# Two norms and the memory values of a decoder layer, reordered around one ring of weight slots

## The chip, the cores and the metric

The kernel runs on one core of a Trainium2 chip. A core has a matrix engine (PE; its weight loads, PEld, overlap its matmuls), a vector engine (DVE), an activation engine (ACT), a general engine (POOL, which here only issues transfers and clears buffers), and a queue (SP) that issues transfers. The engines run apart and wait for each other on semaphores. The metric is the device time of one execution in microseconds (us), median of several runs.

## The reference, cut to what matters

One decoder layer for 256 prompt tokens and 8 sample tokens (T = 264 columns), width 2048. Three sub-layers, each `x <- x + RMSNorm_post(f(RMSNorm_pre(x)))`:

```python
def rmsnorm(x, g):
    x32 = x.astype(F32)
    y = x32 * lax.rsqrt(jnp.mean(x32 * x32, axis=-1, keepdims=True) + EPS) * g.astype(F32)

def memory_kv(mem, g, w_xkv):
    kv = jnp.einsum('bmd,dn->bmn', rmsnorm(mem, g), w_xkv)
    return kv.reshape(B_, M, 2, X_HEADS, X_HEAD_DIM)

def cross_attn(h, mem_kv, w_xq, w_xo):
    q = jnp.einsum('btd,dn->btn', h, w_xq).reshape(B_, T, X_HEADS, X_HEAD_DIM)
    ...
x = x + rmsnorm(y, n_mix_post)
x = x + rmsnorm(cross_attn(rmsnorm(x, n_x_pre), mem_kv, w_xq, w_xo), n_x_post)
y, new_conv = conv_ffn(rmsnorm(x, n_ffn_pre), w_up, conv_w, conv_b, w_down, conv_hist)
```

The divisor of a norm (one number per token) can be applied before a projection or, since the projection is linear, to its result.

## The kernel before

All projections use fp32 numbers split into a high and a low part (fp32r): a product is three matmuls, high by high, high by low, low by high (lines 572 to 574 of `product`). The 2048 features lie on 128 partitions in 16 tiles (KB = 16), tokens in columns. Weights pass through a ring of three buffers (RING = 3), one *slot* of 1 MB (16 blocks of 128 x 128) each, some 400 slots in a fixed order. For each slot SP loads the raw numbers, ACT makes the high part in two halves (`split_hi`, line 537), DVE the low part in two halves (`split_lo`, line 545), and PE runs its 48 matmuls. The splits for slot s + 3 are issued once slot s has been projected, at a place in the ACT and DVE programs that is written by hand. Every engine's program is in order, so an instruction that waits holds back all behind it.

Three stretches matter here.

*The first norm* (after `mix_out`, before cross attention). PE sums the squares of the mixer's output over partitions with a matrix of ones (`norm`, line 1907), then runs three slots of memory keys (PH_KA). DVE takes the divisor (`rstd`), makes the new residual in groups of four tiles, ACT squares each tile into a ring of three buffers, and PE adds up each square with one full-width fp32 matmul (`norm_sum`, line 1911) between the blocks of the second key slot. Only after that second divisor does DVE multiply the residual by it (line 2638) and ACT and DVE split it into `h_hi` and `h_lo`. The first query slot (PH_XQ 0) waits tile by tile for `h_lo`.

*Cross attention*. A list (X_WORK) puts the pieces of the attention behind the slots u = 0 to 22: 8 query slots, 13 slots of keys and values (PH_KB). Each key or value tile comes out as features by tokens and is turned by PE (`kv_turn`, one tile behind its slot) and copied by DVE (line 2656) into `kvtok2`, token rows that the output needs and that the product with the probabilities reads (pieces "oo").

*The second norm* (before the MLP) already works on the undivided residual: DVE and ACT make `x`, `h_hi`, `h_lo` two tiles at a time, PE runs slots 0 and 1 of the up-projection side by side, tile after tile, with a square's sum (`square_sum`, line 2072, 32 output partitions at 32 * (t % 4)) after each tile from the sixth, and from the eleventh on the third slot ten tiles behind (LAG = 10). The divisor multiplies the results (line 2798). Squares lie in a ring of nine. Ahead of this norm's first sum stand 16 transposes of the convolution's history and their four DVE copies (line 2755).

## Time and profile before

| | |
|---|---|
| median of 3 runs | 2647.24 us (2646.9 to 2647.4) |
| the profiled execution's own time | 2646.98 us, its span 2645.3 us |
| PE busy | 2572.2 us, 97% of the span |
| PEld, DVE, ACT busy | 2483.0, 1601.2, 1254.8 us |
| mean granted PE clock | 0.991 of full |

The span runs from the first to the last instruction; the 1.7 us between it and the execution's time lie around it. A matmul's shown length (0.28 us) is longer than the distance between the starts of two (0.12 us), since they are pipelined: rates are read from starts. A row of a stretch gives its bounds and length, then the busy time (and instructions) of PE, PEld, DVE, ACT and POOL, the granted PE clock as a share of full, the busy share of the transfer engines and GB/s.

### The profile page before, as it was taken

The page shows a single profiled execution, that of the slowest core. Times are in us where ns is not written, and L with a number is a line of the kernel's source. Part 1 is how long each engine was busy: PE and PEld are TensorE (multiplying, and loading weights), DVE is VectorE, ACT ScalarE, POOL GpSimd, SP SyncE. Part 2 cuts the span into 40 slices and gives each one's busy share as a digit, 9 for nine tenths or more (in the row PEclk, how much of TensorE's full clock was granted, in tenths as well). Part 3 has the DMA queues.
Part 4 walks back from the last instruction along what each step waited for, and adds up shares of the span by engine and source line. Part 5 has one row for each costly group of instructions (what it writes and reads, how often), then busy time and mean ns, then how long its engine had stood idle before and what let it go on. Part 6 is the DMA issues. An engine that isn't in the chain of part 4 may idle for free. (4 is left out here: it accounts for less than half of the span.)

```text
span 2645.3 us, 53817 instructions
## 1 busy us (share of the span) xinstructions
PE 2572.2 (97%) x20841; PEld 2483.0 (94%) x20841; DVE 1601.2 (61%) x2439; ACT 1254.8 (47%) x1948; POOL 196.3 (7%) x307
## 2 busy tenths in 40 slices
PE   7999999999999999999999999998999999999997
PEld 5988998999999999999999998987999999999997
DVE  4556565544565555555654657546777765777766
ACT  5465555433444444443443644435545555545553
POOL 1112111000111111100000001410000000000000
PEclk9999999999999999999999999999999999999999
DMA  6789789666888888866666656954566577666563
GB/s 201 217 256 282 235 259 294 173 179 191 238 233 233 234 232 230 222 186 184 175 177 206 189 147 190 306 190 128 144 182 183 151 192 198 175 184 180 157 187 108
DMA packets 855053, 530.96 MB, mean 201 GB/s; under 512 B 13961, under 2 KB 832065, under 8 KB 854135
## 3 DMA queue, kind: packets, MB, share of 16 engines
q1 hardware_dynamic: 822583, 440.07, 60.6%
q0 software_dynamic: 27312, 86.50, 9.4%
q10 hardware_dynamic: 5032, 2.62, 0.4%
q8 instruction: 91, 1.49, 0.2%
q14 instruction: 35, 0.29, 0.0%
HBM read 499.79 MB, written 33.29 MB: 202 GB/s over the span
## 5 line engine op out<-in xcount | busy, mean ns | idle before, releaser
L572 PE MATMUL bank<-h_hi,weights_hi 128*128 128x264 f32 x4624 | 1337.9, 289 | 19.8 <-DVE h_lo L2768 6.8
L545 DVE TENSOR_TENSOR weights_lo<-weights_raw,weights_hi 128x1024 fp32r<-128x1024 f32 x814 | 959.4, 1221 | 616.3 <-ACT weights_hi L537 616.3
L573 PE MATMUL bank<-h_lo,weights_hi 128*128 128x264 f32 x4624 | 1316.5, 285 | 0.0
L574 PE MATMUL bank<-h_hi,weights_lo 128*128 128x264 f32 x4624 | 1315.3, 284 | 0.0
L572 PEld LDWEIGHTS bank<-h_hi,weights_hi 128*128 128x128 f32 x4624 | 877.1, 190 | 46.3 <-issue 24.1
L537 ACT ACTIVATE weights_hi<-weights_raw 128x1024 fp32r<-128x1024 f32 x814 | 813.6, 1050 | 207.9 <-PE bank L574 200.8
L573 PEld LDWEIGHTS bank<-h_lo,weights_hi 128*128 128x128 f32 x4624 | 878.2, 190 | 2.1 <-issue 1.9
L574 PEld LDWEIGHTS bank<-h_hi,weights_lo 128*128 128x128 f32 x4624 | 873.3, 189 | 0.0
L572 PE MATMUL bank<-y_hi,weights_hi 128*128 128x264 f32 x1232 | 351.8, 286 | 8.6 <-DVE y_lo L2546 3.1
L574 PE MATMUL bank<-y_hi,weights_lo 128*128 128x264 f32 x1232 | 350.4, 284 | 0.0
L573 PE MATMUL bank<-y_lo,weights_hi 128*128 128x264 f32 x1232 | 348.9, 283 | 0.0
L572 PEld LDWEIGHTS bank<-y_hi,weights_hi 128*128 128x128 f32 x1232 | 232.4, 189 | 9.5 <-issue 4.2
L573 PEld LDWEIGHTS bank<-y_lo,weights_hi 128*128 128x128 f32 x1232 | 232.6, 189 | 0.0
L574 PEld LDWEIGHTS bank<-y_hi,weights_lo 128*128 128x128 f32 x1232 | 232.6, 189 | 0.0
L1148 ACT ACTIVATE qkv<-bank 128x264 f32<-128x264 f32 x72 | 28.2, 391 | 262.0 <-PE bank L574 252.3
L2798 DVE TENSOR_TENSOR squares<-bank,rstd 128x264 f32<-128x264 f32 x88 | 38.0, 432 | 81.4 <-PE bank L574 76.6
L1148 ACT ACTIVATE y_hi<-ffn_value 128x264 f32 (+1 forms) x44 | 18.7, 425 | 140.2 <-DVE ffn_value L2816 140.2
L572 PE MATMUL bank<-memory_normed_hi,weights_hi 128*128 128x256 f32 x256 | 76.5, 299 | 0.0
L573 PE MATMUL bank<-memory_normed_lo,weights_hi 128*128 128x256 f32 x256 | 72.1, 282 | 0.0
L574 PE MATMUL bank<-memory_normed_hi,weights_lo 128*128 128x256 f32 x256 | 71.5, 279 | 0.0
L1499 ACT ACTIVATE ffn_value<-squares,parameters 128x264 f32<-128x264 f32 x44 | 26.7, 608 | 79.9 <-DVE squares L2798 79.9
L964 POOL DMA_DIRECT2D out_conv_p<-conv_new_rows x1 | 0.8, 783 | 842.2 <-DVE conv_new_rows L2860 842.2
(406 smaller groups left out, 2194.8 us busy)
## 6 DMA issues: line engine op xcount, KB each, us to landing
weights_raw<-in_w_in SPq DMA_DIRECT2D x177, 1024.0 KB, 7.0
weights_raw<-in_w_up SPq DMA_DIRECT2D x88, 1024.0 KB, 5.6
weights_raw<-in_w_down SPq DMA_DIRECT2D x64, 704.0 KB, 4.8
gla_state_sample<-in_state_gla POOLq DMA_DIRECT2D x32, 512.0 KB, 8.3
out_gla_s<-gla_state_sample POOLq DMA_DIRECT2D x32, 512.0 KB, 6.4
weights_raw<-in_w_br_gla SPq DMA_DIRECT2D x16, 1024.0 KB, 6.0
weights_raw<-in_w_mix_out SPq DMA_DIRECT2D x16, 1024.0 KB, 6.1
weights_raw<-in_w_xkv SPq DMA_DIRECT2D x16, 1024.0 KB, 7.0
```

What stands on the lines that cost most here:

```text
L537: nc.scalar.activation(w_hi[:, r, half], raw[:, r, half], ACT.Copy).then_inc(hi_ready, 1)
L545: nc.vector.tensor_tensor(w_lo[:, r, half], raw[:, r, half], w_hi[:, r, half].bitcast(F32), ALU.subtract).then_inc(lo_ready, 1)
L572: nc.tensor.matmul(out, wh, xh, start=first and n == 0, stop=False)
L573: nc.tensor.matmul(out, wh, xl, start=False, stop=False)
L574: mm = nc.tensor.matmul(out, wl, xh, start=False, stop=last and n == len(blocks) - 1)
L964: pool.dma_start(A["conv_p"][0, 0].rearrange("r (t p) -> t r p", p=P), newtok[:, 0:2, :]).then_inc(conv_out, 16)
L1148: return nc.scalar.activation(out, in_, ACT.Copy)
L1499: nc.scalar.activation(c, sqr[:, j % 3, :], ACT.Identity, scale=param(PC_CW + 176 + col, n), bias=param(PC_CB + col, n)).then_inc(S(f"c{j} ...
L2798: nc.vector.tensor_tensor(u, bank[p.outs[j]][:, 0:T], rstd[:, :], ALU.mult).then_inc(evac[p.outs[j]], 1)
```

## The change

Both norms now share one scheme. `residual_slots` on PE runs two slots side by side over the 16 tiles, adds up eight squares after the tenth tile and eight after the sixteenth, and then runs the whole third slot, with the last sum after its fourth block. For the first norm these three are query slots 0 to 2, on the undivided residual; the results of all eight query slots are multiplied by the divisor as DVE takes them from PSUM. The first norm's squares have sixteen buffers, the second's twelve. The post-norm's gain goes into ACT's copy of the mixer's output. The history's transposes move behind the second norm's first sum and their copies to ACT. The value half of `w_xkv` is read in eight slots of 512 rows by 512 columns; `value_slot` takes the memory as the stationary operand and 512 weight columns as the moving one, so that values come out as token rows: no turn, and one copy of 512 columns on ACT and one on DVE after the fourth and the eighth slot. The rest of the kernel is as before.

```diff
 
-            return (sqr, cg, cv)[t % 9 // 3][:, t % 3, :]
+            return (sqr, cg, cv, fsq)[t % 12 // 3][:, t % 3, :]
+
+        def early_square(t):
+
+            return qsq[t // 8][:, t % 8, :] if t < 15 else sqr[:, 0, :]
...
-        PH_KB = Phase(book, KB - KA, ([0, 1, 2] * 5)[:KB - KA], 1)
+        PH_KB = Phase(book, 8 - KA, [0, 1, 2, 0, 1], 1)
+        PH_KV = Phase(book, 8, [2, 0, 1, 2], 1)
...
-            for n in range(KA, KB):
+            for n in range(KA, 8):
                 load(sp, PH_KB, n - KA, 0, wide(A["w_xkv"][0], n))
+            for s in range(8):
+                rows, col = s % 4 * 512, 1024 + s // 4 * 512
+                load(sp, PH_KV, s, 0, [(0, 4, 512, A["w_xkv"][0][rows:rows + 512, col:col + 512])])
...
+            def residual_hi(n, c, g_pre):
+                act.wait_ge(*V_N[n].at(f"x{c}"))
+                for t in (2 * c, 2 * c + 1):
+                    nc.scalar.activation(h_hi[:, t, :], xres[:, t, :], ACT.Copy, scale=param(g_pre, t))\
                         .then_inc(A_N[n](f"hi{t}"), 1)
 
...
+            root(0)
+            for c in range(8):
+                residual_hi(0, c, PC_XPRE)
+                if c:
+                    squares(0, c - 1, 16, early_square)
+                if c in (1, 3, 5):
+                    kv_tile(PH_KA, (1, 3, 5).index(c), (1, 3, 5).index(c))
+            squares(0, 7, 16, early_square)
+            split_hi(act, PH_XQ, 0)
+            root(0, "2")
...
+                    if s % 4 == 3:
+                        act.wait_ge(projected, PH_KV.c(s) + 1)
+                        act.wait_ge(mem_out[s // 4], 16)
+                        b = PH_KV.outs[s // 4 * 2]
+                        copy(kvtok2[:, 0, s // 4 * 512:(s // 4 + 1) * 512], bank[b][:, :]).then_inc(evac[b], 1)
+                        act.wait_ge(*PH_KV.saved(s // 4 * 2))
+                        act.sem_inc(A_KV(f"v{s // 4}"), 1)
+                    split_hi(act, PH_KV, s)
...
+            def history(c):
+                act.wait_ge(*P_H.at(f"h{c}"))
+                copy(hist[:, 4 * c:4 * c + 4, :],
+                     bank[3 + c][:, 0:8 * FT].rearrange("p (r t) -> p r t", r=4)).then_inc(A_H(f"h{c}"), 1)
+            act.wait_ge(mem_out[2], 16)
+            history(0)
+            history(1)
...
-            def norm_sum(n, t):
+            def square_sum(n, t, tile):
+                r = 32 * (t % 4)
                 pe.wait_ge(*A_N[n].at(f"q{t}"))
-                nc.tensor.matmul(bank[7][:, 0:T], ones[:, :], sqr[:, t % 3, :], start=t == 0, stop=t == KB - 1)\
+                nc.tensor.matmul(bank[7][r:r + 32, 0:T], ones[:, 0:32], tile, start=t < 4, stop=t >= KB - 4)\
                     .then_inc(P_N[n](f"s{t}"), 1)
+
+            def residual_slots(n, p, tile):
+
+                def block(j, k):
+                    return product(pe, p, j, j, 0, [H_BLOCKS[k]], fresh=k == 0, first=k == 0, last=k == KB - 1)
+                pe.wait_ge(*V_N[n].at("var"))
+                for k in range(KB):
+                    pe.wait_ge(*V_N[n].at(f"lo{k}"))
+                    for j in range(2):
+                        mm = block(j, k)
+                        if k == KB - 1:
+                            mm.then_inc(projected, 1)
+                    if k == 9:
+                        for t in range(8):
+                            square_sum(n, t, tile(t))
+                for t in range(8, KB):
+                    square_sum(n, t, tile(t))
+                for k in range(KB):
+                    if k == 4:
+                        pe.wait_ge(*V_N[n].at("four"))
+                        nc.tensor.matmul(bank[7][:, 0:T], ones[:, :], acc[:, :], start=True, stop=True).then_inc(P_N[n]("all"), 1)
+                    mm = block(2, k)
+                mm.then_inc(projected, 1)
 
             MEM_BLOCKS = over(hm_hi, hm_lo)
             norm(0, V_OUT["mix_end"].at("acc0"))
             for n in range(KA):
-                if n == 1:
-                    pe.wait_ge(*V_N[0].at("var"))
-                product(pe, PH_KA, n, n, 0, MEM_BLOCKS, cols=NP, after=(lambda t: t and norm_sum(0, t - 1)) if n == 1 else None)\
-                    .then_inc(projected, 1)
-                if n == 1:
-                    norm_sum(0, KB - 1)
+                product(pe, PH_KA, n, n, 0, MEM_BLOCKS, cols=NP).then_inc(projected, 1)
+            residual_slots(0, PH_XQ, early_square)
...
+            def value_slot(s):
+
+                r, g = PH_KV.s(s), s // 4
+                for kk in range(4):
+                    if kk % 2 == 0:
+                        pe.wait_ge(lo_ready, PH_KV.c(s) * 2 + (2 * RING + 1 + kk // 2))
+                    k = s % 4 * 4 + kk
+                    wh, wl = (w[:, r, kk * 512:(kk + 1) * 512] for w in (w_hi, w_lo))
+                    for m in range(2):
+                        if k == 0:
+                            pe.wait_ge(*PH_KV.freed(2 * g + m))
+                        out, rows = bank[PH_KV.outs[2 * g + m]][:, :], slice(m * P, m * P + P)
+                        nc.tensor.matmul(out, hm_hi[:, k, rows], wh, start=k == 0, stop=False)
+                        nc.tensor.matmul(out, hm_hi[:, k, rows], wl, start=False, stop=False)
+                        mm = nc.tensor.matmul(out, hm_lo[:, k, rows], wh, start=False, stop=k == KB - 1)
+                mm.then_inc(projected, 1)
 
             def spread(h, n):
...
             xo_slot(PH_XO_E, 0, 0)
+            xo_slot(PH_XO_E, 1, 0)
+            norm(1, V_OUT["xo_end"].at("acc3"))
             pe.wait_ge(hr_in, 16)
             for c in range(4):
                 for r in range(4):
                     mm = turn(bank[3 + c][:, r * 2 * FT:(r + 1) * 2 * FT], hrows[:, 4 * c + r, :], 2 * FT)
                 mm.then_inc(P_H(f"h{c}"), 1)
-            xo_slot(PH_XO_E, 1, 0)
-            norm(1, V_OUT["xo_end"].at("acc3"))
-
-            def square_sum(t):
-                r = 32 * (t % 4)
-                pe.wait_ge(*A_N[1].at(f"q{t}"))
-                nc.tensor.matmul(bank[7][r:r + 32, 0:T], ones[:, 0:32], square(t), start=t < 4, stop=t >= KB - 4)\
-                    .then_inc(P_N[1](f"s{t}"), 1)
-
-            def up_block(j, n):
-                return product(pe, PH_FFN[0][0], j, j, 0, [H_BLOCKS[n]], fresh=n == 0, first=n == 0, last=n == KB - 1)
-            LAG = 10
-            pe.wait_ge(*V_N[1].at("var"))
-            for n in range(KB):
-                pe.wait_ge(*V_N[1].at(f"lo{n}"))
-                for j in range(2):
-                    mm = up_block(j, n)
-                    if n == KB - 1:
-                        mm.then_inc(projected, 1)
-                if n >= 5:
-                    square_sum(n - 5)
-                if n >= LAG:
-                    up_block(2, n - LAG)
-            for t in range(KB - 5, KB):
-                square_sum(t)
-            for n in range(KB - LAG, KB):
-                if n == KB - LAG + 2:
-                    pe.wait_ge(*V_N[1].at("four"))
-                    nc.tensor.matmul(bank[7][:, 0:T], ones[:, :], acc[:, :], start=True, stop=True).then_inc(P_N[1]("all"), 1)
-                mm = up_block(2, n)
-            mm.then_inc(projected, 1)
+
+            residual_slots(1, PH_FFN[0][0], square)
...
+            def residual(n, g_pre, between):
 
                 def low(c):
+                    for t in (2 * c, 2 * c + 1):
+                        dve.wait_ge(*A_N[n].at(f"hi{t}"))
+                        nc.vector.scalar_tensor_tensor(out=h_lo[:, t, :], in0=xres[:, t, :], scalar=param(g_pre, t),
                                                        in1=h_hi[:, t, :].bitcast(F32), op0=ALU.mult, op1=ALU.subtract)\
+                            .then_inc(V_N[n](f"lo{t}"), 1)
+                root(n, P_N[n].at("sum"))
+                inverse(n)
+                dve.wait_ge(*V_N[n].at("rstd"))
+                for c in range(8):
+                    m, x = merged[:, 2 * c:2 * c + 2, :], xres[:, 2 * c:2 * c + 2, :]
+                    nc.vector.tensor_tensor(m, m, rstd[:, None, :].to_broadcast([P, 2, T]), ALU.mult)\
+                        .then_inc(V_N[n](f"yr{c}"), 1)
                     if c:
                         low(c - 1)
+                    dve.wait_ge(*V_N[n].at(f"yr{c}"))
+                    nc.vector.tensor_tensor(x, x, m, ALU.add).then_inc(V_N[n](f"x{c}"), 1)
+                    if c in between:
+                        split_lo(dve, *between[c])
+                low(7)
+                if 8 in between:
+                    split_lo(dve, *between[8])
+                dve.wait_ge(*P_N[n].at("s15"))
+                nc.vector.tensor_copy(acc[:, :], bank[7][:, 0:T]).then_inc(V_N[n]("four"), 1)
+                root(n, P_N[n].at("all"), "2", 1.0 / (32 * D))
             dve.wait_ge(*A_XT.at("x15"))
+            residual(0, PC_XPRE, {2: (PH_KA, 0), 4: (PH_KA, 1), 6: (PH_KA, 2)})
+            split_lo(dve, PH_XQ, 0)
+            inverse(0, "2")
+            dve.wait_ge(*V_N[0].at("rstd2"))
...
+                    dve.wait_ge(projected, PH_XQ.c(u) + 1)
+                    nc.vector.tensor_tensor(qT[:, u, :], bank[PH_XQ.outs[u]][:, 0:T], rstd[:, :], ALU.mult)\
+                        .then_inc(evac[PH_XQ.outs[u]], 1)
+                    if u:
+                        split_lo(dve, PH_XQ, u)
...
             xo_slot(PH_XO_E, "xo_end", 0, 0)
-            dve.wait_ge(mem_out[2], 16)
-            for c in range(4):
-                dve.wait_ge(*P_H.at(f"h{c}"))
-                nc.vector.tensor_copy(hist[:, 4 * c:4 * c + 4, :],
-                                      bank[3 + c][:, 0:8 * FT].rearrange("p (r t) -> p r t", r=4)).then_inc(V_H(f"h{c}"), 1)
             xo_slot(PH_XO_E, "xo_end", 1, 0)
+            residual(1, PC_FPRE, {8: (PH_XO_E, 1)})
```

How the instructions move. PE at the second norm, before: around the tenth and the last tiles, single sums stand between the blocks (572 to 574 are one block of a slot).

```order
L574 MATMUL bank<-h_hi,weights_lo 128x264
L2072 MATMUL bank<-squares,ones 32x264
L572 MATMUL bank<-h_hi,weights_hi 128x264
L573 MATMUL bank<-h_lo,weights_hi 128x264
L574 MATMUL bank<-h_hi,weights_lo 128x264
L572 MATMUL bank<-h_hi,weights_hi 128x264
L573 MATMUL bank<-h_lo,weights_hi 128x264
L574 MATMUL bank<-h_hi,weights_lo 128x264
L2072 MATMUL bank<-squares,ones 32x264
```

The same place of the changed kernel (573 to 575 are one block, 1922 the sums), the first batch:

```order
L573 MATMUL bank<-h_hi,weights_hi 128x264
L574 MATMUL bank<-h_lo,weights_hi 128x264
L575 MATMUL bank<-h_hi,weights_lo 128x264
L1922 MATMUL bank<-squares,ones 32x264 x3
L1922 MATMUL bank<-ffn_gate,ones 32x264 x3
L1922 MATMUL bank<-ffn_value,ones 32x264 x2
L573 MATMUL bank<-h_hi,weights_hi 128x264
L574 MATMUL bank<-h_lo,weights_hi 128x264
```

Eight sums stand together where one stood; a second batch of eight stands behind the sixteenth tile, ahead of the third slot.

DVE at the first norm, before, from the first divisor on:

```order
L2609 TENSOR_SCALAR rstd<-bank 128x264
L2612 RECIPROCAL rstd<-rstd 128x264
L2618 TENSOR_TENSOR merged<-merged,rstd 128x1056
L2621 SCALAR_TENSOR_TENSOR x_residual<-merged,parameters,x_residual 128x264 x4
...
L545 TENSOR_TENSOR weights_lo<-weights_raw,weights_hi 128x1024 x2
L2609 TENSOR_SCALAR rstd<-bank 128x264
L2612 RECIPROCAL rstd<-rstd 128x264
L2638 TENSOR_TENSOR merged<-x_residual,rstd 128x1056 x2
```

And in the changed kernel, from the third pair of tiles to the split of the second key slot, and from the last pair to the third query (546 is a weight split, 2739 a query's multiplication, 2671 the copy of a turned key tile):

```order
L2653 TENSOR_TENSOR x_residual<-x_residual,merged 128x528
L546 TENSOR_TENSOR weights_lo<-weights_raw,weights_hi 128x1024 x2
L2648 TENSOR_TENSOR merged<-merged,rstd 128x528
L2640 SCALAR_TENSOR_TENSOR h_lo<-x_residual,parameters,h_hi 128x264 x2
L2653 TENSOR_TENSOR x_residual<-x_residual,merged 128x528
L2648 TENSOR_TENSOR merged<-merged,rstd 128x528
L2640 SCALAR_TENSOR_TENSOR h_lo<-x_residual,parameters,h_hi 128x264 x2
L2653 TENSOR_TENSOR x_residual<-x_residual,merged 128x528
L546 TENSOR_TENSOR weights_lo<-weights_raw,weights_hi 128x1024 x2
```

```order
L2628 TENSOR_SCALAR rstd<-bank 128x264
L546 TENSOR_TENSOR weights_lo<-weights_raw,weights_hi 128x1024 x2
L2633 RECIPROCAL rstd<-rstd 128x264
L2673 MEMSET x_probs_sample_apart 128x128
L2674 MEMSET x_o_sample_tokens 128x256
L2675 TENSOR_REDUCE sum_of_column_tiles<-identity 128x8
L2678 CAST sample_onehot<-identity 8x8
L2739 TENSOR_TENSOR xq<-bank,rstd 128x264
L2671 COPY mem_kv_tokens<-bank 128x2x128
L2739 TENSOR_TENSOR xq<-bank,rstd 128x264
L546 TENSOR_TENSOR weights_lo<-weights_raw,weights_hi 128x1024 x2
L2671 COPY mem_kv_tokens<-bank 128x2x128
```

The pass of line 2638 over the residual is gone, the weight splits now stand inside the residual's loop, and between the second divisor and the second turned key tile stand two splits.

## Rows read from the trace of the kernel before

**Rows 1.** The page, parts 1 and 5 (costliest groups).

```profile
PE 2572.2 (97%) x20841; PEld 2483.0 (94%) x20841; DVE 1601.2 (61%) x2439; ACT 1254.8 (47%) x1948; POOL 196.3 (7%) x307
...
L545 DVE TENSOR_TENSOR weights_lo<-weights_raw,weights_hi 128x1024 fp32r<-128x1024 f32 x814 | 959.4, 1221 | 616.3 <-ACT weights_hi L537 616.3
...
L537 ACT ACTIVATE weights_hi<-weights_raw 128x1024 fp32r<-128x1024 f32 x814 | 813.6, 1050 | 207.9 <-PE bank L574 200.8
```

**Rows 2.** Stretches: first norm, a part of it, cross attention, second norm.

```profile
1575.60:1628.40 52.80, 47.07 (x331) 44.84 (x329) 42.19 (x62) 26.55 (x52) 5.84 (x8) 0.94 0.49 144
1603.80:1607.10 3.30, 3.29 (x16) 2.98 (x15) 3.30 (x7) 2.71 (x7) 0.00 (x0) 0.50 0.02 5
1628.40:1784.60 156.20, 152.49 (x1264) 141.87 (x1262) 86.24 (x229) 63.01 (x122) 44.27 (x61) 1.00 0.83 251
1819.40:1867.70 48.30, 37.92 (x247) 29.75 (x245) 31.76 (x53) 24.27 (x52) 0.00 (x0) 0.89 0.24 66
```

**Rows 3.** Timeline, PE, first norm: start, length, instruction, idle before and releaser.

```profile
1575.62 0.47 PE L572 MATMUL bank<-memory_normed_hi,weights_hi 128*128 128x256 f32 x1
...
1603.33 0.36 PE L572 MATMUL bank<-h_hi,weights_hi 128*128 128x264 f32 x1 [2.15 <-DVE h_lo L2633]
...
1628.37 0.37 PE L572 MATMUL bank<-h_hi,weights_hi 128*128 128x264 f32 x1
```

**Rows 4.** Timeline, DVE, first norm.

```profile
1580.88 1.26 DVE L2618 TENSOR_TENSOR merged<-merged,rstd 128x1056 f32<-128x1056 f32 x1
```

**Rows 5.** Timeline, DVE, second norm.

```profile
1833.70 0.70 DVE L2773 TENSOR_TENSOR merged<-merged,rstd 128x528 f32<-128x528 f32 x1
...
1835.80 0.70 DVE L2773 TENSOR_TENSOR merged<-merged,rstd 128x528 f32<-128x528 f32 x1
...
1864.11 1.80 DVE L2786 RECIPROCAL rstd<-rstd 128x264 f32<-128x264 f32 x1 [0.49 <-ACT rstd L1479]
...
1866.11 0.37 DVE L2798 TENSOR_TENSOR squares<-bank,rstd 128x264 f32<-128x264 f32 x1
1866.40 2.35 DVE L545 TENSOR_TENSOR weights_lo<-weights_raw,weights_hi 128x1024 fp32r<-128x1024 f32 x2
```

**Rows 6.** Timeline, PE, second norm.

```profile
1834.95 0.56 PE L572 MATMUL bank<-h_hi,weights_hi 128*128 128x264 f32 x1 [5.42 <-DVE h_lo L2768]
...
1859.58 0.63 PE L2072 MATMUL bank<-squares,ones 128*32 128x264 f32 x2
1860.14 0.39 PE L572 MATMUL bank<-h_hi,weights_hi 128*128 128x264 f32 x1
1860.36 0.28 PE L573 MATMUL bank<-h_lo,weights_hi 128*128 128x264 f32 x1
1860.48 0.28 PE L574 MATMUL bank<-h_hi,weights_lo 128*128 128x264 f32 x1
1860.70 0.41 PE L2072 MATMUL bank<-squares,ones 128*32 128x264 f32 x1
1860.70 0.42 PE L2072 MATMUL bank<-ffn_gate,ones 128*32 128x264 f32 x3
...
1861.70 0.39 PE L572 MATMUL bank<-h_hi,weights_hi 128*128 128x264 f32 x1
...
1867.67 0.39 PE L572 MATMUL bank<-h_hi,weights_hi 128*128 128x264 f32 x1 [1.62 <-DVE weights_lo L545]
```

**Rows 7.** Timeline, PE: the history's transposes and the block behind them.

```profile
1819.42 1.38 PE L587 MATMUL bank<-identity,conv_history_rows 88*128 88x88 f32 x16
1820.59 0.37 PE L572 MATMUL bank<-x_o_hi,weights_hi 128*128 128x264 f32 x1
```

**Rows 8.** Groups by form: the turns of values, busy and mean, idle before.

```profile
L587 PE MATMUL bank<-identity,mem_v_tile 128*128 128x128 f32 x16 | 3.1, 274 | 1.6 <-DVE mem_kv_tokens L2656 1.6
```

**Rows 9.** Timeline, PE: ends of a run of 44 matmuls, 256 columns wide.

```profile
1595.84 0.28 PE L573 MATMUL bank<-memory_normed_lo,weights_hi 128*128 128x256 f32 x1
...
1600.90 0.28 PE L574 MATMUL bank<-memory_normed_hi,weights_lo 128*128 128x256 f32 x1
```

**Rows 10.** Timeline, PE: four passes 512 columns wide of unsplit fp32.

```profile
399.06 1.88 PE L1646 MATMUL bank<-gla_v_tokens,gla_k_tokens 128*128 128x512 f32 x4
```

234 lines of the change are left out of this document (86 added, 148 removed).

## The prediction

> **What bounds the kernel now.** I read the page first: PE is busy 97% of the span, the others far less [rows 1]. So time can only come from three places: instructions of PE that go away, PE's idle time, and stretches at the lower clock. Then the stretches that the change touches [rows 2]. The first norm, 52.8 us, has 5.7 us of idle PE and a mean clock of 0.94; cross attention, 156.2 us, has 3.7 us idle and full clock; the second norm, 48.3 us, has 10.4 us idle and a clock of 0.89. The 1 MB slots around them run without a gap, so a slot's start that comes earlier passes on to the end. Last the timelines. In the first norm PE starts the key slots at 1575.62 and the fourth query slot at 1628.37 [rows 3]: 52.75 us for six slots (three of keys, three of queries), the sums and small pieces. In the second norm the first pair of blocks starts at 1834.95 after 5.42 us of idling, and up-projection slot 3 at 1867.67, after 1.62 us of waiting for its own weights' low half [rows 6]. What ends the wait for the first block is DVE's chain there; behind the middle it is PE itself, since the last sum stands at 1861, long after the last low part could have been ready.
>
> **The prices.** A 256-column matmul takes 43 steps in 5.06 us, 0.1177 us each [rows 9]; a 264-column one 0.12 (1860.36 to 1860.48, [rows 6]), so a block of one slot takes 0.36 and a slot 5.75. A lone sum of squares costs 1860.14 - 1859.58 = 0.56 us, and starts 0.22 behind its neighbour where another matmul would start 0.12 behind (1860.48 to 1860.70): 0.66 us in all. Five that stand together cost 1861.70 - 1860.48 - 0.12 = 1.10, and four of them start in the same hundredth [rows 6]: sums on different quarters of the output partitions run together. Eight in a batch are two rounds of four, as five are two rounds; I take 1.15 (bounds: 1.10, and 4.0 if eight went one after another at the 0.5 of a round). DVE needs 2.10 us for one pair of tiles of the residual loop (divide, two low parts, add) and 2.35 for a weight split [rows 5].
>
> **Second norm.** (a) The history's transposes leave the path: 1820.59 - 1819.42 = 1.17 [rows 7]. They go into PE's 5.42 us of idling, ACT's two first copies into ACT's wait for the first residual pair; without that cover they would cost the same 1.2. (b) DVE's weight split moves from the middle of the loop to behind it, so low part 14 is ready 7 x 2.10 after the first one: 1834.8 + 14.7 = 1849.5. PE follows it: two tiles are 1.44 us of blocks against 2.10 of DVE, so even after a start at half clock and 1.15 for the first batch it has caught up by tile 12. Tiles 14 and 15 end at 1851.1, the second batch at 1852.2. (c) The third slot follows, 5.75, with the last sum (0.35) after four blocks: end 1858.3. DVE meanwhile splits the moved weights (1849.9 to 1852.2), then copies the four parts. The sum's result is there at 1854.3; two short operations and the root (1.0), the reciprocal (1.80), the first result's multiplication (its split starts 0.29 behind it) and 1.27 from the split's start to PE's slot 3 [rows 5, 6] give 1858.8. So slot 3 starts at 1858.8 instead of 1867.67: 8.9 us, of which eleven lone sums less what the batches cost are the greater part, and with (a) **10.1**. Its weights' split is again what it waits for, 0.5 us. Bounds: 5 (batches without overlap) and 10.6 (no wait left).
>
> **First norm.** Removed: sixteen full-width sums, DVE's pass over the residual, the wait for the second divisor ahead of all queries. Added: three weight splits inside DVE's loop. That is where PE waits next. From DVE's start at 1580.88 [rows 4]: the first pair's residual is done 1.45 later, each further pair 2.10, each split 2.35 plus about 0.85 in which it waits for ACT, whose high half (1.05 each, [rows 1]) is queued behind that pair's high parts and squares. That puts the first low half of query slot 1 at 1580.88 + 1.45 + 4 x 2.10 + 3.2 + 2.1 = 1595.9, and the last low part of the tiles at 1607.9. PE does the three key slots without a break, 144 x 0.1177 = 17.0, until 1592.6, then one block, then it waits about 2.9 us for query slot 1's weights. Behind this is everything on PE. After a wait of 2.15 us in this kernel the granted clock was 0.50, the lower level of 1.2 GHz, for the 3.3 us from 1603.80 on, 16 matmuls in 3.3 us [rows 2, 3], which at 0.12 would be 1.9: such a fall costs 1.4. With it PE ends tile 15 at 1609.7, the batch at 1610.9, the third slot with its sum at 1617.0. DVE has the last sum at 1612.9, then a split (2.35), the reciprocal (1.80), four small preparations (0.5), query 0 (0.35), a copy, query 1, a second split (2.35), a copy: 1621.7. PE's turn of key tile 2 waits for that last copy, and query slot 3 stands behind the turn. So PE waits twice, 1.4 and 2.7 us, and starts query slot 3 at 1622.1, with a second fall as if at 1623.6. Against 1628.37: **4.8**. Bounds: 8 (neither fall, waits a little shorter) and 0 (DVE and ACT each lose another 2.5 us in their new order). Without the two falls the term would be 4.8 + 2.8 = 7.6, if PE's own time decided throughout. The Trainium skill ("TensorE: Matmul & The Clock Gate", section "HAM oscillation") speaks against this part: a PE that stalls between bursts drops its clock and pays again for warming up. The trace agrees with it in its 0.50.
>
> **Values.** Before, 8 slots of 48 matmuls of 256 columns; now 8 of 24 of 512, as many columns. The trace has no split-fp32 matmul 512 wide. Lower bound 512 columns at the full clock of 2.4 GHz, 0.2133; upper bound 2 x 0.1177 = 0.2354. A 256-wide one stands 0.011 above its own 0.1067; if that extra is per instruction and partly hidden, 0.219: 192 x 0.0164 = 3.1 us (0 to 4.2). The Trainium skill gives N / 2.4 plus 2.5 ns for the spacing (same page, section "Back-to-back issue gap"), 215.8 ns for 512, and by it this term would be 3.8; but for 256 it gives 109, where the trace has 117.7. The turns are 16 matmuls busy 3.1 us [rows 8], at least 16 x 0.12 = 1.9 of the path; I take 2.3. The last turn waited 1.6 for DVE's copy of the one before [rows 8]; no turn, no wait, and the new wait in its place (piece "oo" of head 2 for both copies of the eighth slot) has three pieces with 20 full fp32 matmuls ahead of it on PE, against two copies side by side, each twice as wide as the 264 columns that take DVE 0.37. Sum **7.0**. Eight DVE and eight ACT copies fewer, eight query multiplications moved from ACT to DVE at 0.37: both have room in this stretch, 86 and 63 of 156 us busy, and so does the transfer share of 0.83 [rows 2], which loses small packets. If that cover failed each late slot would cost its own delay.
>
> **Against.** The gain's multiplication makes one ACT copy on the path to the first norm's sum longer: 0.1.
>
> **Sum.** 10.1 + 4.8 + 7.0 - 0.1 = 21.8, from the profiled execution's own 2646.98: 2625.2. The median shown is 0.26 higher: 2625.4.
>
> **The rivals.**
> *R1, batched sums do not overlap as five did.* For it: there is one such place in the trace. Then each of the four batches costs 4.0 instead of 1.15, 11.4 in all, of which some 1.5 fall into PE's waits for DVE: 2625.4 + 9.9 = 2635. Against it: the four equal starts.
> *R2, the first norm gives nothing back.* DVE's chain there is long, every split needs ACT in between, and PE's three waits could each be 1.5 us longer: 2625.4 + 4.8 = 2630. For it: the order is dense; against it: the loop's pace is measured in the second norm.
> *R3, slower than before.* The value matmuls run at the pace of unsplit fp32. Four passes 512 wide lie 0.43 apart (1.88 less one length of 0.59, over three steps) [rows 10]. Then 192 x (0.43 - 0.219) = 40.5 us are added: 2666. It decides from 0.33 us a matmul on (21.8 / 192 = 0.114 above 0.219). Against it: the split ones 256 and 264 wide go at about one column per cycle of the full clock.
> *R4, better.* No clock falls, value matmuls at their bound: 2.8 + 1.1 less: 2621.5.
>
> **How the numbers follow.** Forecast, 2620 to 2629: 0.72. R1 0.08, R2 (2629 to 2634) 0.09, R3 0.03, R4 0.05 (within the range below), and 0.03 for a place that I have not seen and that eats all but nothing. The range for 8 in 10 takes in the forecast, R4 and R2 and reaches to R1: 2618 to 2635. A measurement of this kernel can tell 0.2% (5.3 us) from no change: faster by more 0.94, within 0.02, slower 0.04.
>
> **What will show it.** Second norm: two batches of eight sums, each about 1.15 us from block to block, and 24 us instead of 32.7 from the first block to slot 3. First norm: PE idle near 2.9 us after the third key slot, released by a weight split, and twice ahead of the turns of key tiles 1 and 2, released by DVE's copies, with the clock at 0.5 behind them; query slot 3 some 47 us after the first key slot instead of 52.75. Values: 512-wide matmuls 0.213 to 0.225 us apart and no wait at "oo". The forecast is wrong if the batches take over 2 us, if the 512-wide step is over 0.235, or if a later slot waits for weights that were not late before.

## The result and the profile after

| | before | changed |
|---|---|---|
| median | 2647.4 us (5 runs, 2646.9 to 2649.12) | 2634.22 us (5 runs, 2632.28 to 2634.82) |
| ratio, 95% interval | | 0.9945 (0.9934 to 0.9956) |
| the profiled execution's own time, its span | 2646.98, 2645.3 us | 2634.22, 2632.6 us |

The kernel became 13.2 us faster, where 21.8 were forecast. 2634.22 lies inside the range for 8 in 10 (2618 to 2635) but outside the forecast's own bracket (2620 to 2629, given 0.72). Of all executions below, one of the kernel before, beside the last two experiments, was a slow one (4204.38 us at a mean clock of 0.558) and is left out of every median and interval. The first part of the profile's page after, against [rows 1]: 8.4 us less of busy PE, 206 matmuls fewer, DVE and ACT nearly as before.

```profile
PE 2563.8 (97%) x20635; PEld 2470.2 (94%) x20635; DVE 1596.0 (61%) x2430; ACT 1253.0 (48%) x1938; POOL 195.8 (7%) x307
```

The way to read such a change is by stages. I take five starts on PE that both kernels have and cut the trace there: first key slot, end of the eight queries, the second norm's first sum, its first block, and the first results that DVE takes out of it. Windows of before between these:

```profile
1575.62:1661.08 85.46, 79.73 (x592) 76.74 (x591) 61.07 (x110) 39.95 (x71) 11.61 (x16) 0.96 0.62 181
1661.08:1828.60 167.52, 161.47 (x1348) 151.20 (x1346) 92.83 (x215) 74.66 (x149) 38.51 (x53) 1.00 0.75 231
1828.60:1834.95 6.35, 0.93 (x2) 0.32 (x3) 4.82 (x7) 4.02 (x6) 0.00 (x0) 0.53 0.14 33
1834.95:1866.11 31.16, 29.73 (x178) 22.37 (x178) 19.52 (x34) 13.91 (x33) 0.00 (x0) 0.93 0.12 34
```

The same four of the changed kernel:

```profile
1576.45:1658.61 82.16, 75.76 (x594) 72.61 (x593) 58.32 (x110) 36.68 (x64) 11.58 (x16) 0.94 0.66 190
1658.61:1822.96 164.35, 158.96 (x1124) 139.69 (x1122) 90.24 (x206) 73.17 (x142) 38.43 (x53) 0.99 0.70 232
1822.96:1829.57 6.61, 3.52 (x18) 2.97 (x19) 4.83 (x7) 4.72 (x8) 0.00 (x0) 0.51 0.33 92
1829.57:1852.05 22.48, 21.74 (x168) 19.56 (x169) 19.58 (x35) 14.49 (x35) 0.00 (x0) 0.92 0.17 48
```

The gains are 3.30, 3.17, -0.26 and 8.68 us. The MLP behind takes 756.53 and 756.54. Two differences of these two executions are left. The first key slot started 0.83 later (1576.45 against 1575.62), from the program's first part, which the change does not touch. And behind the last sum the changed kernel took 24.01 us against 22.66: of the last transposes, which are the same in both, those of the changed one ran at the lower clock. Before, then changed, on PE (start, length, instruction, idle before):

```profile
2635.72 1.53 PE L587 MATMUL bank<-identity,x_residual 128*128 128x128 f32 x12 [0.93 <-DVE x_residual L2621]
```

```profile
2608.59 0.71 PE L1917 MATMUL bank<-squares_sum,ones 128*128 128x264 f32 x2 [1.58 <-DVE squares_sum L2849]
...
2621.66 2.75 PE L588 MATMUL bank<-identity,x_residual 128*128 128x128 f32 x12 [1.94 <-DVE x_residual L2871]
2625.17 2.82 PE L588 MATMUL bank<-identity,x_residual 128*128 128x128 f32 x12 [0.76 <-DVE x_residual L2871]
```

3.30 + 3.17 - 0.26 + 8.68 - 0.01 - 0.83 - 1.35 = 12.7, the difference of the spans. The change itself is worth 14.9 by its stages; the rest is what one execution differs by from another.

*First norm.* The changed kernel on PE, against [rows 3]: the wait for query slot 1's weights, the first batch, and the turns of key tiles 0 to 2 with query slot 3 behind them.

```profile
1596.70 0.39 PE L573 MATMUL bank<-h_hi,weights_hi 128*128 128x264 f32 x1 [2.57 <-DVE weights_lo L546]
...
1605.35 1.10 PE L1922 MATMUL bank<-xq_squares,ones 128*32 128x264 f32 x16
...
1618.36 0.38 PE L588 MATMUL bank<-identity,mem_k_a 128*128 128x128 f32 x2
1620.05 0.41 PE L588 MATMUL bank<-identity,mem_k_a 128*128 128x128 f32 x2 [1.30 <-DVE mem_kv_tokens L2671]
1622.98 0.66 PE L588 MATMUL bank<-identity,mem_k_a 128*128 128x128 f32 x2 [2.53 <-DVE mem_kv_tokens L2671]
1623.44 0.64 PE L588 MATMUL bank<-identity,xq 128*8 128x128 f32 x2
1623.72 0.57 PE L573 MATMUL bank<-h_hi,weights_hi 128*128 128x264 f32 x1
1624.09 0.42 PE L574 MATMUL bank<-h_lo,weights_hi 128*128 128x264 f32 x1
1624.31 0.42 PE L575 MATMUL bank<-h_hi,weights_lo 128*128 128x264 f32 x1
...
1631.67 0.28 PE L575 MATMUL bank<-h_hi,weights_lo 128*128 128x264 f32 x1
```

The last matmul of query slot 3 in the kernel before, whose first is at 1628.37 in [rows 3]:

```profile
1634.14 0.28 PE L574 MATMUL bank<-h_hi,weights_lo 128*128 128x264 f32 x1
```

All three waits are where they were forecast (2.57 for 2.9, 1.30 for 1.4, 2.53 for 2.7). Behind the last, matmuls start 0.22 us apart instead of 0.12: the clock is at 0.5. From its first start to its last, slot 3 takes 7.95 us (1623.72 to 1631.67) instead of 5.77 (1628.37 to 1634.14). So the fall costs 2.2 in this slot, where 1.4 was counted, and a few tenths more in the turns ahead of it. The window of slot 3 has a mean clock of 0.70.

```profile
1623.60:1631.90 8.30, 8.30 (x52) 8.11 (x49) 2.51 (x4) 0.38 (x1) 0.00 (x0) 0.70 0.99 252
```

The first norm of the kernel before had a second fall too, behind a wait of 2.05 us for a low part, which the prediction doesn't name:

```profile
1613.95:1617.30 3.35, 3.35 (x17) 3.35 (x16) 3.35 (x7) 2.29 (x3) 2.84 (x4) 0.50 1.14 317
```

Both of its falls are 3.4 us long, and so is the first of the changed kernel. The second of the changed kernel lasts twice as long, 1621.69 to 1628.52.

The weight splits inside DVE's loop are as forecast too, each behind 0.80 us of waiting for ACT, against [rows 4]:

```profile
1581.65 0.71 DVE L2648 TENSOR_TENSOR merged<-merged,rstd 128x528 f32<-128x528 f32 x1
...
1588.11 2.36 DVE L546 TENSOR_TENSOR weights_lo<-weights_raw,weights_hi 128x1024 fp32r<-128x1024 f32 x2 [0.80 <-ACT weights_hi L538]
...
1595.42 2.36 DVE L546 TENSOR_TENSOR weights_lo<-weights_raw,weights_hi 128x1024 fp32r<-128x1024 f32 x2 [0.80 <-ACT weights_hi L538]
```

*Values.* PE of the changed kernel, against [rows 8, 9]: from the second to the last matmul of one value slot, then the turn of the first probabilities (the piece that waits for x_probs) and the next slot.

```profile
1698.83 0.39 PE L1977 MATMUL bank<-weights_lo,memory_normed_hi 128*128 128x512 f32 x1
...
1703.92 0.40 PE L1978 MATMUL bank<-weights_hi,memory_normed_lo 128*128 128x512 f32 x1
...
1706.75 0.89 PE L588 MATMUL bank<-identity,x_probs 128*128 128x128 f32 x4 [0.74 <-DVE x_probs L2703]
1707.29 0.77 PE L1976 MATMUL bank<-weights_hi,memory_normed_hi 128*128 128x512 f32 x1
1707.87 0.63 PE L1977 MATMUL bank<-weights_lo,memory_normed_hi 128*128 128x512 f32 x1
1708.29 0.63 PE L1978 MATMUL bank<-weights_hi,memory_normed_lo 128*128 128x512 f32 x1
```

22 steps in 5.09 us are 0.2314 us a matmul, close to the upper bound of 0.2354 and far from the 0.219 taken. And there is a wait of 0.74, behind which the steps are 0.43: the clock fell in the middle of attention. The same piece in the kernel before waited 0.22 us, and attention stayed at full clock throughout ([rows 2]):

```profile
1709.22 0.66 PE L587 MATMUL bank<-identity,x_probs 128*128 128x128 f32 x4 [0.22 <-DVE x_probs L2688]
```

*Second norm.* Here the forecast holds. PE of the changed kernel, against [rows 6, 7]:

```profile
1823.93 2.55 PE L588 MATMUL bank<-identity,conv_history_rows 88*128 88x88 f32 x16
1829.57 0.56 PE L573 MATMUL bank<-h_hi,weights_hi 128*128 128x264 f32 x1 [3.08 <-DVE h_lo L2640]
...
1839.36 0.28 PE L575 MATMUL bank<-h_hi,weights_lo 128*128 128x264 f32 x1
1839.58 0.42 PE L1922 MATMUL bank<-squares,ones 128*32 128x264 f32 x3
...
1840.61 0.39 PE L573 MATMUL bank<-h_hi,weights_hi 128*128 128x264 f32 x1
...
1845.68 0.28 PE L575 MATMUL bank<-h_hi,weights_lo 128*128 128x264 f32 x1
...
1846.92 0.39 PE L573 MATMUL bank<-h_hi,weights_hi 128*128 128x264 f32 x1
...
1853.60 0.39 PE L573 MATMUL bank<-h_hi,weights_hi 128*128 128x264 f32 x1
```

Eight sums cost 1840.61 - 1839.36 - 0.12 = 1.13 and 1846.92 - 1845.68 - 0.12 = 1.12 us. From the first block to slot 3 it takes 24.03 us where the kernel before took 32.72.

### The profile page after: what moved, and what is told of

Its sections match the earlier page's. It is cut to its first block and busy times, and to the rows that moved or that the text cites. A ratio compares the mean times of both kernels' runs of the same rounds, so it can differ in the third digit from the quotient of the medians.

```text
span 2632.6 us, 53359 instructions
## 1 busy us (share of the span) xinstructions
PE 2563.8 (97%) x20635; PEld 2470.2 (94%) x20635; DVE 1596.0 (61%) x2430; ACT 1253.0 (48%) x1938; POOL 195.8 (7%) x307
## 5 line engine op out<-in xcount | busy, mean ns | idle before, releaser
L2591 DVE TENSOR_TENSOR squares_sum<-squares_sum,squares 128x264 f32<-128x264 f32 x32 | 13.9, 433 | 61.9 <-ACT squares L1314 59.5
L1312 ACT ACTIVATE merged<-bank,parameters 128x264 f32<-128x264 f32 (+1 forms) x32 | 15.4, 482 | 68.7 <-PE bank L575 68.7
L881 POOL DMA_DIRECT2D scratch_dil_q<-qkv_sample x24 | 12.8, 532 | 473.2 <-DVE qkv_sample L2361 423.0
```

Source lines behind the costliest of these rows:

```text
L881: pool.dma_start(d_q[ds(h, 1), g].rearrange("a b e -> (a b) e"), qkvs[:, g, 0:E]).then_inc(dq_st, 16)
L1312: nc.scalar.activation(merged[:, ds(n, 1), :], out[:, None, :], ACT.Copy, scale=scale)
L2591: nc.vector.tensor_tensor(acc[:, :], acc[:, :], sqr[:, k % 3, :], ALU.add).then_inc(V_OUT[S](f"acc{k}"), 1)
```

## The experiments

All ten experiments (one is a repeat of the changed kernel) run on one core, five times each, beside nine executions of the kernel before on the same chip; the last two ran on another chip than the other eight. Totals of one kernel differ by 2 to 5 us between executions, those of the kernel before by up to 11, so the stages of the profiled execution are read beside them. The table has, for each, where the first key slot starts, the stages as above (a: keys and queries; b: the rest of cross attention; c: the sum until the first block; d: until DVE takes the first results), and the time behind the last norm's sum.

| kernel | start | a | b | c | d | tail | median | ratio to before (95%) |
|---|---|---|---|---|---|---|---|---|
| before | 1575.62 | 85.46 | 167.52 | 6.35 | 31.16 | 22.66 | 2647.4 | |
| changed | 1576.45 | 82.16 | 164.35 | 6.61 | 22.48 | 24.01 | 2634.22 | 0.9945 (0.9934-0.9956) |
| old_values | 1577.70 | 82.08 | 169.04 | 6.13 | 22.48 | 22.78 | 2639.86 | 0.9962 (0.9948-0.9975) |
| second_only | 1576.48 | 85.46 | 166.68 | 6.14 | 22.48 | 22.72 | 2638.42 | 0.9955 (0.9941-0.9968) |
| lone_sums | 1575.98 | 82.13 | 164.38 | 6.62 | 27.22 | 22.70 | 2637.25 | 0.9951 (0.9938-0.9965) |
| halves | 1575.44 | 82.02 | 164.99 | 6.14 | 22.49 | 22.64 | 2632.66 | 0.9936 (0.9923-0.995) |
| changed_again | 1575.68 | 82.07 | 164.37 | 6.67 | 22.50 | 22.72 | 2633.8 | 0.9946 (0.9933-0.996) |
| turns_late | 1577.73 | 77.12 | 162.73 | 6.14 | 22.49 | 23.99 | 2626.76 | 0.9917 (0.9903-0.993) |
| pt0_late | 1576.12 | 82.10 | 162.96 | 6.14 | 22.48 | 22.66 | 2630.96 | 0.9936 (0.9922-0.995) |
| slot_ahead | 1575.44 | 79.93 | 162.76 | 6.47 | 22.49 | 23.82 | 2629.55 | 0.9931 (0.9918-0.9945) |
| three | 1575.92 | 76.08 | 162.93 | 6.14 | 22.49 | 23.11 | 2626.65 | 0.9911 (0.9894-0.9928) |
| five | 1578.06 | 75.48 | 162.59 | 6.14 | 22.48 | 22.72 | 2623.99 | 0.9903 (0.9886-0.992) |

The medians of before beside them were 2649.34 (old_values to halves), 2648.14 (changed_again to slot_ahead) and 2649.62 us (three, five). Where neither a stage nor the time of its start is changed, a, b and d repeat within 0.2 us from kernel to kernel; c lies between 6.13 and 6.67, starts lie between 1575.4 and 1578.1, tails between 22.6 and 24.0.

**The values alone undone.** `PH_KB` has its thirteen slots again, `value_slot` and its copies are gone.

```diff
-        PH_KB = Phase(book, 8 - KA, [0, 1, 2, 0, 1], 1)
-        PH_KV = Phase(book, 8, [2, 0, 1, 2], 1)
+        PH_KB = Phase(book, KB - KA, ([0, 1, 2] * 5)[:KB - KA], 1)
```

> The changed kernel with the value half as before: thirteen slots of key and value tiles of 256 columns, each turned by PE and copied by DVE; both norms as changed. Theory A (the values term was mis-sized): the new form saves 0.9 us of matmuls (192 x (0.2354 - 0.231)), about 2 us of turns and 0.6 us of waits, and gives back about 1.5 us through a longer wait for x_probs and the fall of the clock behind it, so this kernel is 2 us slower than the changed one: 2636. Theory B (the term of 7.0 us holds and something else in cross attention was disturbed by the new first norm): 7 us slower, 2641. The trace tells too: by A the wait for x_probs ahead of the first turn of probabilities is about 0.2 us again and the granted clock behind it stays full; by B it is long here too.

The median is 2639.86, between the two theories, and stage b is 4.7 us longer than in the changed kernel. But the expected sign of A, a short wait for x_probs, isn't there: PE waited 1.84 us for it. ACT and PE of this kernel show where that begins:

```profile
1683.31 2.01 ACT L537 ACTIVATE weights_hi<-weights_raw 128x1024 fp32r<-128x1024 f32 x2 [3.15 <-DMA weights_raw<-in_w_xkv]
```

```profile
1692.84 0.66 PE L587 MATMUL bank<-identity,x_probs 128*128 128x128 f32 x4 [1.84 <-DVE x_probs L2672]
```

A slot's weights landed late, ACT's split waited 3.15 us for them, DVE's chain of cached products behind its own split came late, and PE paid. The granted clock stayed at 1.00 behind these 1.84 us. With this kernel's waits in attention (4.2 us for x_probs, tiles, scores and sample queries, against 2.1 before) down to 2.1, stage b would be 166.9 and the two forms differ by 2.6 us, near A's 2; with it, the change of the values saves 4.7. Neither theory was whole. Late weights are no accident of this one execution: ACT waits for a value slot's weights in all three traces of the old form, 1.44 us in that of second_only and 0.85 in that of the kernel before, and in none of the nine of the new form.

```profile
1691.25 2.01 ACT L537 ACTIVATE weights_hi<-weights_raw 128x1024 fp32r<-128x1024 f32 x2 [0.85 <-DMA weights_raw<-in_w_xkv]
```

Around that place the transfer engines of the kernel before have no room, though the mean of 0.83 in [rows 2] suggests some:

```profile
1640.00:1700.00 60.00, 59.74 (x499) 56.58 (x499) 33.28 (x85) 26.11 (x43) 28.54 (x40) 1.00 1.00 308
```

In the same 60 us of the changed kernel, counted from the first key slot, the share is 0.94. So some of what the new form gains may come from its transfers, with rows of 512 columns instead of 128, and not from PE's instructions; no experiment changes the one without the other.

**The second norm alone.** The kernel before with the new second norm.

```diff
-                if c == 3:
-                    split_lo(dve, PH_XO_E, 1)
             low(7)
+            split_lo(dve, PH_XO_E, 1)
...
-            xo_slot(PH_XO_E, 1, 0)
-            norm(1, V_OUT["xo_end"].at("acc3"))
...
+            residual_slots(1, PH_FFN[0][0], square)
```

> The kernel before with the second norm of the changed one alone: two batches of eight sums, twelve buffers of squares, third slot behind them, history's transposes behind the first sum and their copies on ACT, the weight split behind the residual loop. Theory A (the second norm's term holds as forecast, near 10): 2647.4 - 9.7 = 2637.7, with 24.0 us from the first block to slot 3 and the transposes' 1.2 us gone from the path. Theory B (part of what was read there came from the state in which cross attention leaves DVE and ACT in the changed kernel): a gain of 6 or less, 2641 or more.

Stage d is 22.48, to the hundredth that of the changed kernel, b is 0.84 and c 0.21 shorter: 9.7 us, as A has it. The median, 2638.42, gives 10.9 against the 2649.34 beside it. So the part is worth its term by itself, within what the executions of the kernel before differ by.

**Sums one by one, in the second norm.**

```diff
-                    if k == 9:
+                    if n == 0 and k == 9:
                         for t in range(8):
                             square_sum(n, t, tile(t))
-                for t in range(8, KB):
+                    if n == 1 and k >= 5:
+                        square_sum(n, k - 5, tile(k - 5))
+                for t in range(8 if n == 0 else KB - 5, KB):
                     square_sum(n, t, tile(t))
```

> The changed kernel, but in the second norm each sum of squares stands alone behind a tile from the sixth on, eleven in all, and the last five together; the third slot still follows behind. Theory A (a lone sum costs 0.66 us, eight in a batch 1.10): from the sixth tile on PE needs 11 x 0.72 + 11 x 0.66 + 1.10 = 16.3 us where the changed kernel took 10.9 with 0.74 us of waits, so slot 3 starts 5.4 us later and the kernel is 5 to 5.5 us slower: 2639.5. Theory B (the gain of the second norm lies in the third slot standing last and the split behind the loop, and lone sums fall into PE's waits for DVE): 0 to 2 us slower, 2634 to 2636.

Stage d grows by 4.74 us, a little under the 5.0 to 5.5 of A and far over B. The median, 2637.25, is only 3.0 above that of the changed kernel, with 1.3 of the difference in the tail. PE has no gap left in stage d:

```profile
1829.11:1856.33 27.22, 27.22 (x168) 20.73 (x169) 19.59 (x35) 14.49 (x35) 0.00 (x0) 0.93 0.14 39
```

So more than half of what stage d gained (8.68) is that eight sums stand together.

**Value matmuls in halves.**

```diff
-                        nc.tensor.matmul(out, hm_hi[:, k, rows], wh, start=k == 0, stop=False)
-                        nc.tensor.matmul(out, hm_hi[:, k, rows], wl, start=False, stop=False)
-                        mm = nc.tensor.matmul(out, hm_lo[:, k, rows], wh, start=False, stop=k == KB - 1)
+                        for x in (slice(0, 256), slice(256, 512)):
+                            nc.tensor.matmul(out[:, x], hm_hi[:, k, rows], wh[:, x], start=k == 0 and x.start == 0, stop=False)
+                            nc.tensor.matmul(out[:, x], hm_hi[:, k, rows], wl[:, x], start=False, stop=False)
+                            mm = nc.tensor.matmul(out[:, x], hm_lo[:, k, rows], wh[:, x], start=False, stop=k == KB - 1 and x.start > 0)
```

> The changed kernel with each 512-wide value matmul issued as two of 256 columns, 384 instead of 192. Theory A (the extra over the bound of columns at the full clock goes almost wholly with the columns: 0.0178 us at 512 and 0.011 at 256): the pair costs 0.2354 instead of 0.231, 0.85 us in all: 2635.1, within 0.1% of the changed kernel. Theory B (what the forecast assumed, an extra per instruction that a wide matmul halves to reach 0.219): 192 x 0.0164 = 3.1 us slower, 2637.3. Read from the trace: the distance of two starts.

PE of this kernel, 24 steps of 256 columns from the first row to the last:

```profile
1698.86 0.28 PE L1977 MATMUL bank<-weights_hi,memory_normed_hi 128*128 128x256 f32 x1
...
1701.68 0.28 PE L1977 MATMUL bank<-weights_hi,memory_normed_hi 128*128 128x256 f32 x1
```

2.82 / 24 = 0.1175 each, 0.235 a pair, against 0.2314 for one of 512. 192 x (0.235 - 0.2314) would be 0.7 us, and the waits for x_probs are 0.2 shorter (0.65 and 0.10 us against 0.73 and 0.21). Stage b grows by 0.6 us (164.37 to 164.99), a little more than this leaves. A holds: going from 256 to 512 columns saves 0.004 us a matmul, not 0.016. The median, 2632.66, is no slower than the changed kernel's, since 0.6 us is less than executions differ by.

**The changed kernel again.**

> The changed kernel itself once more, as the measure for the other three on the same chip. From its first key slot to the first slot of keys behind the queries it took 82.16 us, from there to the second norm's first sum 164.35, from that norm's first block to the first query of up-projection results 22.48, and from the last norm's sum to the end 24.01, where three other kernels with the same code there took 22.64 to 22.78. Theory A: the first three come again within 0.3 us, and what differs between executions lies ahead of the first norm (its start has been anywhere from 1575.1 to 1577.4) and in that last stretch, where a fall of the clock is a matter of chance: 22.7 or 24.0. Theory B: the last stretch is 24.0 whenever this kernel runs, a consequence of the change.

Stages a, b and d come within 0.1 us, the tail is 22.72 instead of 24.01. A holds: the tail's clock differs from one execution to another. Its five times (2632.07, 2632.22, 2633.8, 2634.2, 2635.07) are as wide as such a fall and the differing start make them.

**Key turns later.**

```diff
-                    if u < KA:
-                        kv_turn(u)
+                    if KA <= u < 2 * KA:
+                        kv_turn(u - KA)
...
-                    if u < KA:
-                        kv_turned(u)
+                    if KA <= u < 2 * KA:
+                        kv_turned(u - KA)
```

> The changed kernel with the turns of the first three key tiles (and their DVE copies) behind query slots 3, 4 and 5 instead of behind slots 0 to 2. Theory A (slot 3 stood behind two waits of 1.30 and 2.53 us for DVE's copies, and ran 2.4 us longer at the lower clock because of them): slot 3 now waits only until DVE has taken query 0 out of its bank, about 1.2 us, and starts 4 us earlier; if the clock falls all the same, 4.0 in all, if not, 6.4: 2628 to 2630. Theory B (the transfers, busy 0.97 of the stretch behind in the kernel before, are the floor there): the slots behind wait for weights that are late and most of it is lost, 0 to 2 us gained, with ACT's weight splits idle behind a transfer of weights and PE's waits behind that.

Stage a loses 4.95 us, b another 1.6, the median 7.0. The clock doesn't fall ahead of slot 3 any more:

```profile
1621.35 0.38 PE L588 MATMUL bank<-identity,xq 128*8 128x128 f32 x2 [1.54 <-DVE xq L2739]
1621.48 0.37 PE L573 MATMUL bank<-h_hi,weights_hi 128*128 128x264 f32 x1
```

So the two waits for DVE's copies, with what they did to the clock, cost the changed kernel 4.95 us more than the one of 1.54 that stands here now: slot 3 starts 3.5 us earlier after the first key slot and takes 5.77 us again, and the three turns cost 0.22 each where they stand now. Transfers are not the floor here (B falls): neither ACT nor DVE waits for a transfer in these stages. That b is shorter too was not expected: its waits are the same (0.7 for x_probs), yet the clock stays full behind them. The twenty microseconds in question, in the changed kernel and here:

```profile
1698.61:1718.61 20.00, 19.26 (x110) 14.73 (x109) 14.48 (x50) 7.43 (x16) 7.89 (x11) 0.91 0.71 252
```

```profile
1694.85:1714.85 20.00, 19.26 (x117) 14.84 (x116) 14.95 (x52) 7.98 (x18) 8.76 (x13) 1.00 0.75 253
```

**The first probabilities' turn later.**

```diff
-                  11: "kb1 qs2 pt0", 12: "sm1 ka2 sc1",
+                  11: "kb1 qs2", 12: "pt0 sm1 ka2 sc1",
```

> The changed kernel with one piece of the attention moved: the turn of the first probabilities stands behind the following slot's 24 matmuls instead of ahead of them. Theory A (the shorter slots of values made this piece wait 0.74 us for DVE's x_probs, and the clock fell behind it, 1.4 us): both go, 2.1 us faster, and the mean clock of the twenty microseconds in question is 1.00 instead of 0.91: 2632. Theory B (DVE's chain of cached products sets the pace there, so the wait turns up at the next piece that needs DVE): 0 to 0.5 us.

Stage b loses 1.4 us. (Stage c is 0.5 shorter as well, but it is 6.14 in seven of these kernels and 6.5 to 6.7 in the rest, whatever their edit.) The mean clock of the stretch is 1.00 again. But of the 0.74 us nothing is won: 0.9 us of waiting for ACT's copy of these turned probabilities stands one piece later. So what was won is the fall of the clock and not the wait; A and B each had half.

**Slot 0 ahead of slot 1.**

```diff
                 for k in range(KB):
+                    if n == 0 and k < 8:
+                        continue
+                    if n == 0 and k == 8:
+                        for j in range(2):
+                            for kk in range(8):
+                                if j == 0:
+                                    pe.wait_ge(*V_N[n].at(f"lo{kk}"))
+                                block(j, kk)
                     pe.wait_ge(*V_N[n].at(f"lo{k}"))
```

> The changed kernel, where in the first norm query slot 0 runs its first eight tiles alone before slot 1 starts, so that PE has 2.9 us of blocks to do while it would wait 2.57 us for slot 1's weights; the rest is the same. Theory A (DVE's loop ends 1.1 us ahead of PE only because the wait and the clock's fall put PE behind): the wait and the fall go, PE follows DVE's last low part directly, and all behind it is 1.1 to 1.7 us earlier, less what PE then waits tile by tile; the two waits at the key turns move with DVE and stay. 2633. Theory B (DVE's chain up to the second divisor and the copies is the limit of all that follows, from its own work alone): 0 us, the waits at the turns grow by what was gained.

Stage a is 2.1 us shorter, a little over A's 1.7. PE's wait for slot 1's weights is all but gone (0.03 us); instead it waits 2.15 us for low part 12, without a fall of the clock, and the turns' waits stay (1.31 and 2.53):

```profile
1605.16 0.39 PE L573 MATMUL bank<-h_hi,weights_hi 128*128 128x264 f32 x1 [2.15 <-DVE h_lo L2648]
...
1617.98 0.41 PE L588 MATMUL bank<-identity,mem_k_a 128*128 128x128 f32 x2 [1.31 <-DVE mem_kv_tokens L2679]
1620.92 0.66 PE L588 MATMUL bank<-identity,mem_k_a 128*128 128x128 f32 x2 [2.53 <-DVE mem_kv_tokens L2679]
```

A explains half of it. The last of these turns comes 45.48 us after the first key slot instead of 46.53, 1.05 earlier: that is A's DVE chain. The other 1.1 is slot 3 itself, 6.77 us from its first start to its last instead of 7.88, behind the same waits: the clock is back at full at 1623.82, after 3.4 us at half instead of 6.8. A did not have this, and no run shows what decides the length of a fall. The slot's window:

```profile
1621.66:1628.55 6.89, 6.89 (x50) 6.84 (x48) 2.38 (x4) 0.38 (x1) 0.00 (x0) 0.84 1.07 285
```

**All three, and then DVE's order.** The last kernel adds to the three edits:

```diff
-            split_lo(dve, PH_XQ, 0)
             inverse(0, "2")
             dve.wait_ge(*V_N[0].at("rstd2"))
+            query(0)
+            query(1)
+            split_lo(dve, PH_XQ, 0)
```

> The changed kernel with all three edits: turns of key tiles behind query slots 3 to 5, the turn of the first probabilities behind the following slot, query slot 0 eight tiles ahead of slot 1. Theory A (they act on different waits and add up): 4.95 and 2.2 us in the stretch from the first key slot to the keys behind the queries, and behind that 1.4 to 1.6 us once, since the two that start attention earlier had already no fall of the clock there: 8.7 in all, 2625. Theory B (a start 7 us earlier makes the weights' transfers late, as in the kernel with the values as before, where ACT waited 3.15 us for one): 3 us of it are lost again, 2628, with PE waiting for a split behind a transfer.

> The same three edits, and on DVE the reciprocal of the second divisor and the multiplications of queries 0 and 1 ahead of the weight split of query slot 0 instead of behind it. Theory A (query slot 3 waits 1.54 us for DVE to take queries 0 and 1 out of their banks, because the 2.35 us split stands ahead of the reciprocal): the split's first half is what slot 3 waits for now, 0.6 us or less, and 1.0 to 1.5 us are gained over the kernel with three edits: 2624. Theory B (transfers are the floor by now): no gain over it.

With the three edits a and b together lose 7.4 us (of 8.7 by A), and no wait behind a transfer shows; with DVE's order 0.9 more. In both kernels stages a and b run at a mean clock of 1.00. In the last one ACT already waits 5.28 us for the weights of a query slot (at 1626.67); DVE's split behind it waits 1.2 and PE doesn't, so transfers are close to being the floor. Waits and gains don't add up fully, since each edit brings PE sooner to the next thing that DVE is late with. The last kernel, 2623.99 us, has the lowest median here, some 10 us below the changed one and 1.0% below before. The intervals of it and of the three edits overlap, so that the last edit is faster is read from the stages alone.

## Why the prediction was right or wrong

*What bounds the kernel.* Right: every microsecond won at a slot's start went through the MLP to the end (756.53 and 756.54).

*The total.* 13.2 us were measured by the medians (14.3 when the changed kernel ran again), 14.9 by the stages, of 21.8. That the time falls inside the range is in part luck: the range was stretched to 2635 for R1 and R2, and neither is what happened.

*Second norm, 10.1.* Right. Stages b to d of the kernel with this part alone give 9.7. Batches cost 1.13 for 1.15 taken; 24.03 us from block to slot 3 for 24.0; slot 3 waits 0.15 us there, where 0.5 was forecast.

*First norm, 4.8.* The mechanism was right, down to the three waits; stage a gained 3.3. The term that failed is the second fall of the clock, sized at 1.4 like the one at 1603.80 of the kernel before; it lasted twice as long and cost 2.2. Query slot 3 also came 0.8 us later after the first key slot than worked out (47.27 for 46.5). The two make 1.6, where 1.5 were missing. The Trainium skill's warning ("TensorE: Matmul & The Clock Gate", section "HAM oscillation") that a PE which stalls between bursts drops its clock is borne out by these 2.2 us.

*Values, 7.0.* Wrong by 5. Stage b gained 3.17, of which 1.17 is the transposes' term: 2.0. Three steps failed.
1. "if that extra is per instruction and partly hidden, 0.219": it isn't. The step measured 0.2314, so 192 matmuls save 0.8 us for 3.1. The two bounds held the value, the choice between them was wrong. The Trainium skill's N / 2.4 plus 2.5 ns ("TensorE: Matmul & The Clock Gate", section "Back-to-back issue gap") gives 215.8 ns; the trace does not agree with it, and its 231.4 ns decide. The page itself gives that formula for an isolated matmul and 131 ns for a stream of them at 512 columns, with which the trace agrees still less. The sign named for this term, 0.213 to 0.225 us apart, was missed.
2. "both have room in this stretch": by share of busy time, yes. But the first probabilities' turn had waited 0.22 us for DVE before, so that PE and DVE were level there, and now it waits 0.74. The wait at the last turn is gone as forecast, but one of 0.49 for ACT's x_probs_sample_apart has come. Waits fell from 2.1 to 1.5 us, where the removed 1.6 was counted in full. The transfers had no room in 60 of these 156 us (the row of 1640 to 1700 above); the change eased them to 0.94 there.
3. No fall of the clock was counted in attention. The one behind that wait of 0.74 costs 1.4 to 1.6 us (turning it away: 164.37 to 162.96, 162.76 and 162.73).

0.8 for the matmuls, 2.3 for the turns, 0.6 for waits, less 1.6: 2.1, against 2.0 measured. The agreement proves little, since the turns were not measured alone: the key tiles' turns that turns_late moved cost 0.22 us each, by which eight would be an estimated 1.8 and 0.4 of the gain would lack a cause.

*The gain's multiplication, -0.1.* Too small to be told from what starts differ by.

*Rivals.* R1 fell: a batch is 1.1 us. R2 fell: stage a gained 3.3, and the three waits were no longer than forecast; a third of the term was lost all the same, to the longer fall and to a later slot 3. R3 fell: 0.231 us, not 0.43. R4 fell on both counts. Most of the loss came from what none of them had: a longer fall in the first norm, a fall and level engines in attention, beside a matmul step near its upper bound.
